# Level products of a gated recurrence, two chunks to a product: 36 interleaved slots of a tuned two-block transformer kernel become 20

## What is computed

```python
def step(S, inp):
    qb, kb, vb, bb = inp                     # bb: running sum of log f within the chunk
    o_inter = jnp.einsum('bhtk,bhkv->bhtv', qb * jnp.exp(bb), S)
    rel = bb[:, :, :, None, :] - bb[:, :, None, :, :]
    decay = jnp.exp(jnp.where(causal, rel, -jnp.inf))
    A = jnp.einsum('bhtk,bhsk,bhtsk->bhts', qb, kb, decay)
    o = o_inter + jnp.einsum('bhts,bhsv->bhtv', A, vb)
    blast = bb[:, :, -1:, :]
    S_new = jnp.exp(blast[:, :, 0, :])[..., None] * S + jnp.einsum('bhsk,bhsv->bhkv', kb * jnp.exp(blast - bb), vb)
    return S_new, o
```

## Time and profile before

| | us |
|---|---|
| median of 3 runs | 1521.23 |
| lowest, highest | 1520.24, 1522.88 |
| the profiled execution: its own time | 1522.84 |
| the profiled execution: its span | 1521.1 |
| phase a1 with the slots in it, in that span | 71.9 to 190.3 |

### The profile page before, as it was taken

One profiled execution on the slowest core, in us unless ns is written; L12 is line 12 of the kernel. 1 busy time (PEld: TensorE's weight loads), 2 busy tenths in 40 slices (PEclk: granted clock), 3 DMA queues, 4 the chain that ended last, 5 costly groups with the idle time before them and its releaser, 6 DMA issues.

```text
span 1521.1 us, 19395 instructions
## 1 busy us (share of the span) xinstructions
PE 1458.6 (96%) x7182; PEld 1169.6 (77%) x7182; DVE 955.3 (63%) x1703; ACT 406.4 (27%) x840; POOL 94.5 (6%) x74
## 2 busy tenths in 40 slices
PE   4999998989999999998999999999998999999997
PEld 3888866768888888886866666778887888888886
DVE  8777697876767675566466666875546444444443
ACT  5323245331111101003244445521113222221011
POOL 0000000020000000233400000000030000000110
PEclk9999999989999999998999999999998999999999
DMA  9343232336555665433221111122322222223322
GB/s 372 108 164 111 88 131 74 125 96 208 190 195 192 194 189 152 154 115 115 70 69 43 43 42 56 42 69 93 107 96 68 94 98 95 97 96 91 104 87 94
DMA packets 52609, 175.79 MB, mean 116 GB/s; under 512 B 5952, under 2 KB 6336, under 8 KB 52544
## 3 DMA queue, kind: packets, MB, share of 16 engines
q1 hardware_dynamic: 52544, 174.94, 35.2%
HBM read 172.82 MB, written 2.10 MB: 115 GB/s over the span
## 4 chain that ended last, share of the span: by engine, by line
PE 52%; ACT 1%; DVE 1%; issue 0%; ACTq 0%; DVEq 0%
PE bank L626 12%; PE bank L628 12%; PE bank L627 11%; PE bank L1093 8%; PE bank L1112 2%; PE bank L1147 2%; PE bank L1124 2%; PE bank L638 1%; PE bank L639 1%; PE bank L640 1%; PE bank L1024 0%; DVE wl L1615 0%; PE bank L1137 0%; PE bank L1068 0%; PE bank L735 0%
## 5 line engine op out<-in xcount | busy, mean ns | idle before, releaser
L626 PE MATMUL bank<-uh,wh 128*128 128x512 f32 x808 | 316.2, 391 | 6.0 <-DVE wl L1615 4.8
L628 PE MATMUL bank<-uh,wl 128*128 128x512 f32 x808 | 315.3, 390 | 0.0
L627 PE MATMUL bank<-ul,wh 128*128 128x512 f32 x808 | 315.0, 390 | 0.0
L1613 DVE CAST wh<-wraw 128x1024 fp32r<-128x1024 f32 (+1 forms) x223 | 148.0, 663 | 193.7 <-PE bank L628 178.5
L1615 DVE TENSOR_TENSOR wl<-wraw,wh 128x1024 fp32r<-128x1024 f32 (+1 forms) x223 | 260.3, 1167 | 7.7
L626 PEld LDWEIGHTS bank<-uh,wh 128*128 128x128 f32 x808 | 152.1, 188 | 38.9 <-issue 4.9
L628 PEld LDWEIGHTS bank<-uh,wl 128*128 128x128 f32 x808 | 151.9, 188 | 31.9
L627 PEld LDWEIGHTS bank<-ul,wh 128*128 128x128 f32 x808 | 152.1, 188 | 31.5
L626 PE MATMUL bank<-hh,wh 128*128 128x512 f32 x352 | 137.6, 391 | 0.0
L628 PE MATMUL bank<-hh,wl 128*128 128x512 f32 x352 | 137.1, 390 | 0.0
L627 PE MATMUL bank<-hl,wh 128*128 128x512 f32 x352 | 137.0, 389 | 0.0
(11 more groups left out here) (340 smaller groups left out, 2294.4 us busy)
## 6 DMA issues: line engine op xcount, KB each, us to landing
ada<-in_w_ada_dram SPq DMA_DIRECT2D x96, 512.0 KB, 4.7
wraw<-in_w_in_dram SPq DMA_DIRECT2D x61, 512.0 KB, 3.4
wraw<-in_w_ffn_gate_dram SPq DMA_DIRECT2D x44, 512.0 KB, 3.3
wraw<-in_w_ffn_up_dram SPq DMA_DIRECT2D x44, 512.0 KB, 3.3
wraw<-in_w_ffn_down_dram SPq DMA_DIRECT2D x32, 512.0 KB, 3.5
wraw<-in_w_ffn_down_dram SPq DMA_DIRECT2D x16, 384.0 KB, 3.1
wraw<-in_w_out_dram SPq DMA_DIRECT2D x16, 256.0 KB, 2.8
wraw<-in_w_out_dram SPq DMA_DIRECT2D x8, 512.0 KB, 3.3
```

The costliest lines, as they stand in the source:

```text
L626: nc.tensor.matmul(bank[:], a, rh[:, k0 + k, :], start=(first and k == 0), stop=False)
L627: nc.tensor.matmul(bank[:], a, rl[:, k0 + k, :], start=False, stop=False)
L628: mm = nc.tensor.matmul(bank[:], b, rh[:, k0 + k, :], start=False, stop=(last and k == nk - 1))
L1613: V.tensor_copy(wh[:, slot, 0:n], wraw[:, slot, 0:n]).then_inc(w_hi, 1)
```

## The change

A level uses half of the queries and half of the keys of a chunk. The changed kernel puts two chunks into one product, so that a step has two products (128x128) in place of four; step 0, the diagonal, keeps its four.

- **Layout.** `drain_turned` lays down the second half of the sequence (tokens 256 to 511) backwards in `p1`, for queries, keys and values, with two ACT instructions of 256 for one of 512. `CHUNK_AT` = [0, 1, 3, 2] says where the four chunks then stand. The heads' outputs are turned back where they are transposed in the attention part: there a transpose writes its PSUM block backwards (`bank[:, ::-1]`).
- **Products.** The stationary operand is `kpk`, the level's keys of both halves, packed by a new ACT instruction `pack_keys(p)` (28 of them, 256 elements), which waits for `grow`; the product waits for it (`g_pack`). The moving operand is read out of `p1` by `queries_of` in three steps: pairs of blocks, the two halves in turn, m elements in a row.
- **Grow and merge.** `grow` has the same two instructions of 256 elements with another walk through memory. A merge of a level takes 256 elements into `amx`; after the last level two predicated copies of 256 (`order`: earlier or later) bring `amx` to `am`. The level masks are no longer ordered, one VectorE instruction less for each of seven; two order masks replace one. One GpSimd memset more clears `amx`.
- **Slots.** 20 slots in place of 36, with both heads' steps in one slot (products 2t and 2t + 1) and five or six tiles behind. In DVE's stream both grows come first, then a split if `SPLIT_AT` has one, both merges, states, and a split if `SPLIT_IN` has one. The last head's output stands in a slot of its own behind all tiles. In ACT's stream the packs come after a slot's drain, rounding and turned copies.

Nothing else changes, the weight units and their loads included. The diff, cut to its core:

```diff
+HALF = T // 2
+CHUNK_AT = [0, 1, 3, 2]
...
+        amx = at("amx", [P, 2, HALF], where=h_at + 15 * K2)
+        kpk = at("kpk", [P, 2, HALF], where=n_at + 4 * K2)
+        order = at("order", [P, 2, P], I32, where=s_at + 8 * K2)
...
-        A1_UNITS, STEPS, SLOTS = len(TILES["a1"]), 8 * HEADS1, 8 * HEADS1 + 4
+        A1_UNITS, STEPS, SLOTS = len(TILES["a1"]), 8 * HEADS1, 4 * HEADS1 + 4
...
-        SPLIT_AT = {done_in(n - 1) + 1: n for n in range(1, A1_UNITS)}
+        SPLIT_IN, SPLIT_AT = {}, {0: 1}
+        for n_ in range(2, A1_UNITS):
+            t_ = done_in(n_ - 1)
+            early = 2 * KT * n_ <= (SLOT_END[t_ - 1] if t_ else KT) + SLOT_END[t_]
+            (SPLIT_IN if early else SPLIT_AT)[t_ if early else t_ + 1] = n_
...
+        MERGED = [p + 1 + sum(1 for _, s_ in STEP_OF[:p + 1] if s_ == 7) for p in range(STEPS)]
...
-        TURN_V, TURN_K = {2: 0, 3: 1, 22: 2, 23: 3}, {16: 0, 18: 1, 31: 2, 33: 3}
-        SUM_U, HEAD_O = {17: 0, 19: 1, 32: 2, 34: 3}, {19: 0, 20: 1, 34: 2, 35: 3}
+        PACKED = [sum(1 for _, s_ in STEP_OF[:p + 1] if s_ < 7) for p in range(STEPS)]
+        TURN_V, TURN_K = {1: 0, 2: 1, 13: 2, 14: 3}, {8: 0, 10: 1, 16: 2, 18: 3}
+        SUM_U, HEAD_O = {9: 0, 11: 1, 17: 2, 19: 3}, {11: 0, 12: 1, 18: 2, 20: 3}
...
+        def keys_of(h, m):
+
+            rows = p1[:, 4 + h:6 + h, :].rearrange("p a t -> p (a t)")[:, 0:2 * (HALF + m)]
+            halves = rows.rearrange("p (j r) -> p j r", j=2)[:, :, 0:HALF]
+            return halves.rearrange("p j (n b i) -> p j n b i", b=2, i=m)[:, :, :, 0, :].rearrange("p j n i -> p n j i")
+
+        def queries_of(h, m, c):
+
+            rows = p1[:, h:h + 2, :].rearrange("p a t -> p (a t)")[:, c * P + m:c * P + m + 2 * (HALF - m)]
+            halves = rows.rearrange("p (j r) -> p j r", j=2)[:, ::-1, 0:P]
+            return halves.rearrange("p j (n b i) -> p j n b i", b=2, i=m)[:, :, :, 0, :].rearrange("p j n i -> p n j i")
...
+            nc.gpsimd.memset(amx[:], 0.0).then_inc(g_cleared, 1)
...
                 else:
                     pe.wait_ge(g_q, GROWN[p - 2])
-                for c in range(NT):
+                    pe.wait_ge(g_pack, PACKED[p - 2])
+                for c in range(2 if s_ else NT):
                     cc = slice(c * P, (c + 1) * P)
-                    mm = nc.tensor.matmul(B[4 + p % 4][:, cc], p1[:, 4 + h, cc], p1[:, h, cc], start=True, stop=True)
+                    m = SPANS[s_ - 1]
+                    mm = nc.tensor.matmul(B[4 + p % 4][:, cc], kpk[:, h % 2, cc] if s_ else p1[:, 4 + h, cc],
+                                          queries_of(h, m, c) if s_ else p1[:, h, cc], start=True, stop=True)
...
+            for t in range(SLOTS + 1):
+                for p in (2 * t, 2 * t + 1):
+                    if p < STEPS:
+                        level_products(p)
...
+                if t in HEAD_O:
+                    head_output(HEAD_O[t])
+                if t < SLOTS:
+                    a1_tiles(SLOT_END[t - 1] if t else KT, SLOT_END[t])
...
-                    turn_mix(spare(m), p1[:, 8 + HG_AT[m], :])
+                    for n, c in enumerate(CHUNK_AT):
+                        bank = spare(m)[:, n * P:(n + 1) * P]
+                        mm = nc.tensor.transpose(bank if c < 2 else bank[:, ::-1],
+                                                 p1[:, 8 + HG_AT[m], c * P:(c + 1) * P], ident[:])
...
+            def drain_turned(tile, bank, func):
+
+                A(p1[:, tile, 0:HALF], bank[:, 0:HALF], func)
+                A(p1[:, tile, HALF:T], bank[:, HALF:T][:, ::-1], func).then_inc(drain_a, 1)
...
+            def pack_keys(p):
+
+                h, s_ = STEP_OF[p]
+                if s_ == 0:
+                    act.wait_ge(g_k, h + 1)
+                    if h >= 2:
+                        act.wait_ge(g_p, LAST_STEP[h - 2] + 1)
+                else:
+                    act.wait_ge(g_q, GROWN[p])
+                m = SPANS[s_]
+                A(kpk[:, h % 2, :].rearrange("p (n j i) -> p n j i", j=2, i=m), keys_of(h, m), ACT.Copy).then_inc(g_pack, 1)
...
-                sp_ = spans(h, m)
-                for tile, own, other in ((q, 1, 0), (k, 0, 1)):
-                    part = tile.rearrange("p (n a m) -> p n a m", a=2, m=m)[:, :, own, :]
-                    V.tensor_tensor(part, part, sp_[:, :, other:other + 1].broadcast_to([P, T // (2 * m), m]),
-                                    ALU.mult).then_inc(g_q, 1)
+                n, d = HALF // m, DOFF[m]
+                late = p1[:, h, m:T - m].rearrange("p (j g i) -> p j g i", j=2, i=m)[:, :, 0:n - 1:2, :]
+                soon = fd[:, h, d:d + 2 * n + 2].rearrange("p (j g) -> p j g", j=2)[:, :, 0:n:2]
+                V.tensor_tensor(late, late, soon.unsqueeze(3).broadcast_to([P, 2, n // 2, m]), ALU.mult).then_inc(g_q, 1)
+                rows = p1[:, 4 + h:6 + h, :].rearrange("p a t -> p (a t)")[:, 0:T + 2 * m]
+                soon = rows.rearrange("p (j g i) -> p j g i", j=2, i=m)[:, :, 0:n:2, :]
+                late = fd[:, h, d + 1:d + 2 * n - 1].rearrange("p (j g) -> p j g", j=2)[:, :, 0:n - 1:2]
+                V.tensor_tensor(soon, soon, late.unsqueeze(3).broadcast_to([P, 2, n // 2, m]), ALU.mult).then_inc(g_q, 1)
...
                 h, s_ = STEP_OF[p]
                 if p >= 2:
-                    v.wait_ge(g_a, p - 1)
...
+                both = amx[:, h % 2, :].rearrange("p (c t) -> p c t", c=2)
+                V.copy_predicated(both, lmask[:, 7 - s_, :].unsqueeze(1).broadcast_to([P, 2, P]),
+                                  B[4 + p % 4][:, 0:HALF].rearrange("p (c t) -> p c t", c=2)).then_inc(g_a, 1)
+                if s_ == 7:
+                    v.wait_ge(g_a, MERGED[p] - 1)
+                    for j in range(2):
+                        mm = V.copy_predicated(am[:, h, j * HALF:(j + 1) * HALF].rearrange("p (c t) -> p c t", c=2),
+                                               order[:, j, :].unsqueeze(1).broadcast_to([P, 2, P]), both)
+                    mm.then_inc(g_a, 1)
...
+            for t in range(SLOTS):
+                if t < STEPS // 2:
+                    grow(2 * t)
+                    grow(2 * t + 1)
+                if t in SPLIT_AT:
+                    split_next(SPLIT_AT[t])
+                if t < STEPS // 2:
+                    merge(2 * t)
+                    merge(2 * t + 1)
+                if t in SUM_U:
+                    states(SUM_U[t])
+                if t in SPLIT_IN:
+                    split_next(SPLIT_IN[t])
```

127 lines of the change are left out of this document (60 added, 67 removed).

## The result

| | before | after |
|---|---|---|
| median, runs | 1520.74 us, 4 | 1509.45 us, 4 |
| lowest, highest | 1520.13, 1522.88 | 1508.54, 1510.76 |
| profiled execution: own time, span | 1522.84, 1521.1 | 1509.58, 1507.5 |
| stage a1: first tile to first attention score | 72.09 to 190.29: 118.20 | 71.65 to 178.05: 106.40 |
| from that score to the end of the span | 1330.81 | 1329.45 |

The changed kernel is 0.8% faster: the ratio is 0.9923 (95% interval 0.9910 to 0.9935). Forecast were 1510.1 us and a range of 1507.5 to 1518.0. Between the two spans lie 13.6 us: 11.8 in the stage, 1.4 behind it, and 0.4 ahead of it, where nothing changed for TensorE. The medians of these four runs each are 11.3 apart; over all runs on record (37 of before, 9 changed) they are 1521.23 and 1509.33, 11.9 apart. The profiled execution of before lay 1.6 above the median given ahead of the forecast.

The account below looks back on a forecast made before the run. TensorE, busy 96% of the span, was taken as the bound. Products -12.5, two waits -0.6 and new waits +2.0 sum to -11.1 us: 1511.7 from the profiled 1522.84, median 1510.1, range 1507.5 to 1518.0.

Parts of the forecast that it names:

- The term that carries it: TensorE's level products in stage a1: fewer instructions at 0.111 us each, 28.5 us down to 16.0, a gain of 12.5.
- Reads in pieces: Level products' moving operand via queries_of: scattered reads taken as free, since a float32 instruction takes 0.10 whatever it moves.
- The upper end: Level products: if scattered reads set the 0.110, 0.116 us more on each of 112 instructions, 13.0 us.
- Waits for packs: TensorE before products 22 and 23: waits of 1.2 and 0.2 us, plus 0.6 added, 2.0 us lost.
- VectorE runs without a gap from 1.9 us into slot 7: VectorE's walk towards slot 11: grows of slot 9 end 14.1 us after slot 7 began, making TensorE wait.
- The 0.6 that I added for restarts and close slots: TensorE in the slots: 0.6 us for its restarts and slots that come close (5, 10, 18).
- the 0.6 for the two waits: End of the stage: TensorE's waits for the squares (0.2) and at the first attention fill (0.4) go.
- the 1.5 us that I had named as a sign of error: After the first attention score: forecast wrong if the span there differs from before by over 1.5 us.
- B (scattered reads): Level products: scattered reads cost TensorE; half price gives 1514.8 us, full price 1521.3. Chance 0.14.
- C (a longer chain): Grow, pack, product: packs of 0.5 and grow halves of 0.4 us cost 6 us of waits, 1514.1. Chance 0.12.
- D: VectorE's grow halves and half merges: full width paid for instructions over two halves, +6.4 us, 1527.6. Chance 0.07.
- E: Attention part: starts earlier but waits for something unmoved, giving the gain back; full price 1521.2 us. Chance 0.05.

Follow-up runs that it names:

- plain reads: Changed kernel with level products reading a plain block of queries, so other numbers result; stage 105.84 us against 106.40.
- packed queries: Changed kernel with ScalarE also packing the queries for m = 1; stage 105.90 us, 1508.71 us in 5 runs, ratio to before 0.9921.
- packs or merges twice: Two runs on the changed kernel: every pack made twice, stage 107.59 us; every level merge made twice, stage 108.56 us; extra copies go unread.
- the split first: Changed kernel with VectorE making the SPLIT_AT splits and their modulations ahead of the slot's grows; stage 107.43 us.
- Products apart: Changed kernel with three tiles between the first and the second head's products in each slot; stage 109.61 us.
- 36 slots: New layout, packs and products in the 36 slots of the kernel before, one head's step each; stage 106.97 us, 1511.52 us, ratio to before 0.9932.
- four products again: Changed kernel with two more plain, unread products in each level step; stage 118.86 us, 1521.48 us in 10 runs, ratio to before 1.0003.

## Why the prediction was right

**The term that carries it held.** 112 instructions fewer at 0.111: forecast -12.5, measured 12.46 by the experiment that gives them back. Blocks of 0.89 and of 1.78 for the diagonals (114.54 to 116.32) came as worked out from one block of before.

**Reads in pieces: the step that failed was "a float32 instruction takes 0.10 whatever it moves".** Forecast 0, measured 1.0 us in 32 of the 112 instructions. The 62-column row hid the price, by this estimate: at 0.164 for 128 columns a scattered column costs 1.28 ns; 62 of them are 0.08 us, less than the 0.10 that even one column takes. So the row most likely showed a floor and not the price of a scattered read; no run has scattered reads of fewer columns to test it. The upper end (13.0, the full doubling of all widths) was far off too, since from m = 4 on nothing is paid. The rule that the forecast quoted, from the Trainium skill, "Advanced Engine Details and Errata", section "SBUF Cachelines", is nearer. By it only m = 1 should pay; the trace agrees that m = 1 pays nearly all of it, at 1.47 times the plain instruction, so 0.86 us, not the 1.8 of a doubling. At m = 2, with two hits on a line, the rule has no penalty, and the measurement has a small one (0.96 for 0.89); the measurement decides.

**Waits for packs: forecast 2.0, measured 0.** The only wait left is for `states`, which the forecast did not have. The place was right: slot 11 waits as soon as TensorE comes earlier (0.41 with plain reads, 0.3 with packed queries). It is not alone: with packs or merges twice slot 5 waits as well, with the split first slot 6. What was off was the sentence "VectorE runs without a gap from 1.9 us into slot 7". With plain reads, which is the case I walked, slot 7 starts at 109.95 and the split at 110.92, 0.97 into it. From there on the walk holds: in the changed kernel 12.1 us from the split's start in slot 7 (111.17) to the end of the grows of slot 9 (123.28), walked 12.2; and 7.1 from there to the end of the pack (130.37), walked 7.1. VectorE of the changed kernel at the end of it:

```profile
126.81 1.23 DVE L1915 TENSOR_TENSOR wl<-wraw,wh 128x1024 fp32r<-128x1024 f32 x1 [1.81 <-ACT wh L1380]
127.95 1.28 DVE L1691 CUSTOM_DVE_ANT_0 ada<-ada,scb,vt 128x1024 f32<-128x1024 f32 x1
...
129.16 0.42 DVE L1951 TENSOR_TENSOR p<-p,fd 128x256 f32<-128x256 f32 x1
129.50 0.42 DVE L1955 TENSOR_TENSOR p<-p,fd 128x256 f32<-128x256 f32 x1
...
130.50 0.77 DVE L1968 COPY_PREDICATED amx<-lmask,bank 128x256 f32<-128x256 int32 x2
```

So the walk's durations were right from slot 7 on and its start was 0.9 too late. A half merge holds VectorE for 0.33 and not 0.36, but VectorE stands idle at two places ahead of slot 7 (1.45 us before 87.91, 1.36 before 96.65, with plain reads), and what it gains before these need not reach slot 7. Where the 0.9 lies in slots 0 to 6 stays open. The 0.6 that I added for restarts and close slots appeared nowhere. The forecast also halved 20 drains; the code halves 12, four of them in the stage, so ScalarE rose there by 9.7 us and not by 13, which changed nothing in the sum.

**The misses cancel, in part by a coupling and for the rest by luck.** The slow blocks at m = 1 and 2 stand ahead of the tight slot. Those of the first pair of heads hold up the packs as well, those of the second pair do not, so of their 1.0 us the packs gain about 0.5, as the experiment with plain reads shows (0.56 of 1.0 arrives). Had I priced the reads right and walked again, 1.0 would have been added and about 0.5 would have gone off the waits. The other 1.5 us too much in the waits have nothing to do with the reads; that they outweigh what the reads cost is luck. In the stage the forecast's terms come to -10.7 and the traces have -11.8.

The sum of the stage by its terms, all by starts: -12.46 + 1.00 + 0.04 (waits: 0.42 for the squares before, 0.46 for `states` now) = -11.4; the traces have -11.8. The 0.4 left lies where TensorE changes between tile passes and float32 products, which it did 36 times before and does 20 times now. Added over the stage, what the passes and products take beyond 0.227 and 0.111 us each, without waits and slow reads, is 0.4 less. Most of it stands in the first passes behind a block (0.232 a pass for the second and third, 0.227 further on). So such a change costs TensorE 0.02 to 0.03 us of its own. Products apart and 36 slots, with 36 changes each, have 0.5 and 0.3 more than the changed kernel; four products again, with 20, has none, and its stage is therefore 0.7 over before and not 1.1. Why a change costs this, no run shows. The forecast had nothing for it.

**Behind the stage.** Of the 0.6 for the two waits the 0.4 at the first attention fill went as forecast. TensorE's waits from the first score to the last attention output, before and after:

```profile
PE bank L911 <- ACT wt L1386: 6.0, 5, 2.9
PE bank L950 <- issue: 1.4, 1, 1.4
PE bank L950 <- ACT p L1417: 1.0, 1, 1.0
```

```profile
PE bank L941 <- ACT wt L1442: 6.0, 5, 2.9
PE bank L984 <- issue: 1.4, 1, 1.4
PE bank L984 <- ACT p L1473: 0.2, 1, 0.2
```

That part of the program takes 86.3 us in both profiles of the changed kernel and 87.2 and 87.0 in those of before, all four at a mean granted clock of 0.94 there. So 0.8 of the 1.4 repeats. Half of that is the fill's 0.4, which 36 slots with the new products have again. The drain's wait (L1417 before, L1473 after) is also shorter: 1.0 and 0.7 before, 0.2 and none after. But it goes with the clock as well: it is 0 to 0.6 in the seven changed kernels whose clock is 0.94 in this part, and 1.0 in the four where it is 0.96. I had not foreseen it, and no run separates the two. The backward transposes cost nothing that shows there, as taken. The rest of the difference behind the stage is smaller than what the same program shows between chips. So the 1.5 us that I had named as a sign of error was kept, with 1.4, but not by much.

**The rivals.** B (scattered reads) was real at 1.0 of its 13.0 us: the mechanism exists, its size was that of neither end. C (a longer chain) is excluded by the packs at 436 ns and grow halves at 419, and because packs run twice cost 1.2. D fell with the rows of the grow halves: full width would be 688 ns, as the step-0 multiplication takes, and they take 419. E fell with the table above: the gain of the stage arrives at the end.

## What to carry to other kernels

Where one engine is busy all the time, count its instructions first: the gain here is 112 times 0.111 us to within 0.7, and the reordering around it is worth 0.6. Before a row is taken as the price of an access pattern, ask whether it lies at a floor: a short instruction can hide in its fixed cost what a long one pays, and a row with as many columns as the new instruction was needed. Two terms of a sum that act on the same chain must be walked together: delaying the engine that waits shortens its wait, as far as the same delay does not reach the engine it waits for. And a total that agrees says little on its terms: here three were off by 0.4 to 2.0 us.

## What was not expected of the hardware

A float32 product of 128 columns takes 0.111 us with the moving operand in a row or in pieces of four elements and more; 0.120 in pieces of two; 0.164 in single elements. The pieces come in turn from the two halves of the sequence; whether their size or this alternation sets the price, no run separates. A change between passes of 512 columns and float32 products of 128 costs 0.02 to 0.03 us. ScalarE reads PSUM backwards at the forward rate (378 ns for 256 elements), but its copy that gathers every second run costs 436. VectorE's predicated copy costs 444 ns for 256 elements and 747 for 512, whether the mask picks a level or a half.
